# Down weights of the expert pairs issued from ACT's DMA queue, gate and up weights from SyncE's, in place of both from one queue

## What is computed

```python
def hier_moe(h, ...):     # 4 groups x 8 experts; top-1 group, then top-2 experts in it
    ...
    combine = jnp.sum(jax.nn.one_hot(eid, N_EXPERTS) * top_w[..., None], axis=1)
    a = jnp.einsum('cd,edf->cef', tc, w_g)      # w_g: 32 experts x 1024 x 256
    u = jnp.einsum('cd,edf->cef', tc, w_u)
    z = jax.nn.silu(a) * u * combine[..., None]
    return jnp.einsum('cef,efd->cd', z, w_d)    # w_d: 32 experts x 256 x 1024
```

## Time and profile before

| | before |
|---|---|
| median of 3 runs | 1402.3 us (1400.13 to 1407.38) |
| the profiled execution: its own time | 1399.06 us |
| its span, first to last instruction | 1397.4 us |
| PE busy | 1231.0 us, 88% |
| DVE, ACT, POOL busy | 586.8, 412.2, 239.1 us |
| DMA queue q1 (SP) | 281.57 MB, 52.5% of 16 engines' span |
| q0 (POOL), q10 (ACT) | 23.25 MB, 0.76 MB |
| mean granted PE clock | 0.961 |

### The profile page before, as it was taken

How to read it: one execution, slowest core, us unless ns; L and a number is a source line. 1 busy time by engine, 2 the same in 40 slices (tenths; PEclk the granted TensorE clock), 3 DMA queues, 4 the chain that set the end, 5 groups by cost and what they waited for, 6 DMA issues and landing times.

```text
span 1397.4 us, 18940 instructions
## 1 busy us (share of the span) xinstructions
PE 1231.0 (88%) x6424; PEld 809.6 (58%) x6425; DVE 586.8 (42%) x1353; ACT 412.2 (29%) x761; POOL 239.1 (17%) x183
## 2 busy tenths in 40 slices
PE   5999987999988998888499999789999889987871
PEld 5877766788876433333177777567888744332320
DVE  4467677333335222111254677753232442221115
ACT  5334444433342110001153443443332411110003
POOL 0314140022101111111003232301121011111100
PEclk9999999999999999999899999999999999998996
DMA  4423220453545999999533222105537289999995
GB/s 187 129 89 93 76 91 1 151 208 108 181 166 190 413 423 424 425 421 406 217 123 117 85 85 93 57 16 196 180 106 266 81 304 408 425 423 423 419 373 203
DMA packets 68192, 306.79 MB, mean 220 GB/s; under 512 B 11888, under 2 KB 11888, under 8 KB 56832
## 3 DMA queue, kind: packets, MB, share of 16 engines
q1 hardware_dynamic: 56960, 281.57, 52.5%
q0 software_dynamic: 10992, 23.25, 4.4%
q10 hardware_dynamic: 144, 0.76, 0.1%
HBM read 290.33 MB, written 23.07 MB: 224 GB/s over the span
## 4 chain that ended last, share of the span: by engine, by line
PE 60%; DMA 15%; SPq 7%; DVE 7%; issue 4%; ACT 3%; DVEq 2%; ACTq 0%; POOL 0%; POOLq 0%
PE bank L463 13%; PE bank L465 12%; PE bank L464 12%; PE bank L742 9%; DMA gu<-in_gu_w 9%; SPq L349 4%; PE bank L758 4%; SPq L354 3%; DMA raw<-in_stream 2%; PE bank L598 2%; DVEq L1186 2%; PE bank L737 1%; ACT prob L949 1%; PE bank L534 1%; DVE prob L1209 1%
## 5 line engine op out<-in xcount | busy, mean ns | idle before, releaser
L742 PE MATMUL bank<-gu,xgt 128*64 128x512 f32 x1024 | 242.4, 624 | 43.0 <-DMA gu<-in_gu_w 41.1
L463 PE MATMUL bank<-h_hi,w_hi 128*128 128x512 f32 x640 | 253.9, 397 | 6.6 <-DVE h_lo L1146 3.6
L465 PE MATMUL bank<-h_hi,w_lo 128*128 128x512 f32 x640 | 250.3, 391 | 0.0
L464 PE MATMUL bank<-h_lo,w_hi 128*128 128x512 f32 x640 | 249.8, 390 | 0.0
L742 PEld LDWEIGHTS bank<-gu,xgt 128*64 128x64 f32 x1024 | 75.6, 143 | 205.7 <-issue 188.7
L1104 DVE TENSOR_TENSOR w_lo<-raw,w_hi 128x1024 fp32r<-128x1024 f32 x102 | 128.0, 1255 | 149.6 <-ACT w_hi L868 148.6
L463 PEld LDWEIGHTS bank<-h_hi,w_hi 128*128 128x128 f32 x640 | 120.6, 188 | 33.0 <-DVE h_lo L1146 4.0
L465 PEld LDWEIGHTS bank<-h_hi,w_lo 128*128 128x128 f32 x640 | 120.5, 188 | 25.6
L464 PEld LDWEIGHTS bank<-h_lo,w_hi 128*128 128x128 f32 x640 | 120.6, 188 | 24.0
L868 ACT ACTIVATE w_hi<-raw 128x1024 fp32r<-128x1024 f32 x102 | 107.5, 1054 | 57.3 <-PE bank L465 57.3
L758 PE MATMUL bank<-dn,zt 128*64 128x512 f32 x512 | 117.2, 599 | 6.7 <-ACT zt L1065 3.2
(11 more groups left out here) (172 smaller groups left out, 1624.0 us busy)
## 6 DMA issues: line engine op xcount, KB each, us to landing
gu<-in_gu_w SPq DMA_DIRECT2D x18, 4096.0 KB, 33.2
raw<-in_stream SPq DMA_DIRECT2D x112, 512.0 KB, 3.3
dn<-in_dn_w SPq DMA_DIRECT2D x18, 2048.0 KB, 34.4
gu<-in_gu_w SPq DMA_DIRECT2D x24, 1024.0 KB, 19.5
dn<-in_dn_w SPq DMA_DIRECT2D x20, 1024.0 KB, 18.7
gu<-in_gu_w SPq DMA_DIRECT2D x32, 512.0 KB, 5.7
gu<-in_gu_w SPq DMA_DIRECT2D x8, 2048.0 KB, 24.3
swp<-pj SPq DMA_DIRECT2D x136, 64.0 KB, 2.0
```

The source lines that it names most:

```text
L463: mm(dst, ah, bh, start=start, stop=False)
L464: mm(dst, ah, bl, start=False, stop=False)
L465: return mm(dst, al, bh, start=False, stop=stop)
L742: last = mm(bank[b][e * CAP:(e + 1) * CAP, :], xgt[:, x_s, k, e * CAP:(e + 1) * CAP], gu[w_s][:, e, k, :], start=k == 0, stop=k == KD - 1)
```

## The change

SP no longer issues the down weights of pairs 3 to 15. ACT issues them instead: in its own loop over the pairs, behind the copy `zt` of pair n and before `y_half(n)`, it waits for dn_ok of pair n and issues the down weights of pair n + 3 (one DMA of 2 MB, or two of 1 MB for the pairs in PARTS). The buffers, the sizes, the semaphores that tell of the landing and the conditions under which a load may start are the same. The down weights of pairs 0 to 2 stay with SP.

```diff
@@ SP
-            def load_dn(l, p):
-                s = p % RING
-                sp.dma_start(dn[s]..., dn_w[...]).then_inc(dn_ld[s], 16)
...
                 load_gu_part(l, 3, 0)
                 sp.wait_ge(gu_ok, l * PAIRS + 1)
                 load_gu_part(l, 3, 1)
-                sp.wait_ge(dn_ok, l * PAIRS + 1)
-                load_dn_part(l, 3, 0)
-                load_dn_part(l, 3, 1)
                 for p in range(4, PAIRS):
                     sp.wait_ge(gu_ok, l * PAIRS + p - RING + 1)
                     ...
-                    sp.wait_ge(dn_ok, l * PAIRS + p - RING + 1)
-                    if p in PARTS:
-                        load_dn_part(l, p, 0)
-                        load_dn_part(l, p, 1)
-                    else:
-                        load_dn(l, p)
@@ ACT
+                def load_dn(p):
+                    if p in PARTS:
+                        for f in range(2):
+                            act.dma_start(dn[p % RING][:, :, f, :], dn_w[...]).then_inc(dn_part[p][f], 16)
+                    else:
+                        act.dma_start(dn[p % RING]..., dn_w[...]).then_inc(dn_ld[p % RING], 16)
                 for n in range(PAIRS):
                     ...
                     run(zt[:, :, :], ..., ACT.Copy).then_inc(zte_ok, 1)
+                    if n + RING < PAIRS:
+                        hold(act, dn_ok, n0 + n + 1)
+                        load_dn(n + RING)
                     y_half(n)
```

More of the change, by code:

```diff
@@ L340, in load_gu @@
                              gu_w[bass.ds(l * PAIRS + p, 1), :, :, :].rearrange("o e p n -> p (o e) n")).then_inc(gu_ld[s], 16)
-            def load_dn(l, p):
-                s = p % RING
-                sp.dma_start(dn[s][:, :, :, :].rearrange("p e k n -> p e (k n)"),
-                             dn_w[bass.ds(l * PAIRS + p, 1), :, :, :].rearrange("o e p n -> p (o e) n")).then_inc(dn_ld[s], 16)
             def load_gu_part(l, p, q):
@@ L1059, in y_half @@
                     run(yb[n % 2][:, 0:T], bank[4][:, :], ACT.Copy).then_inc(ya_ok, 1)
+                def load_dn(p):
+                    if p in PARTS:
+                        for f in range(2):
+                            act.dma_start(dn[p % RING][:, :, f, :], dn_w[bass.ds(l * PAIRS + p, 1), :, :, f * D:(f + 1) * D].rearrange(
+                                "o e p n -> p (o e) n")).then_inc(dn_part[p][f], 16)
+                    else:
+                        act.dma_start(dn[p % RING][:, :, :, :].rearrange("p e k n -> p e (k n)"),
+                                      dn_w[bass.ds(l * PAIRS + p, 1), :, :, :].rearrange("o e p n -> p (o e) n")).then_inc(dn_ld[p % RING], 16)
                 for n in range(PAIRS):
```

## The result

The median went from 1400.0 us (18 runs) to 1411.1 us (18 runs), a ratio of 1.0085 with a 95% interval of 1.0072 to 1.0098. The profiled execution went from 1399.06 to 1410.30 us, its span from 1397.4 to 1408.5. The forecast was +9.8 us, and both its sign and its size came about. Half of its reasoning was right; the profile after shows that the other half was not.

The account below looks back on a forecast made before the run. The prediction took the full-rate weight stream and PE's tail to bound each expert half. Its terms, 0 + 0 + 4.8 + 5.0 = +9.8 us, took 1402.3 to 1412.1 us, with a range of 1400.5 to 1421.

Parts of the forecast that it names:

- A full stream sets the end of the expert half: Expert halves: PE loses its lead and waits for weights; the end follows from the full-rate weight stream and PE's tail.
- SP's long issues are worth nothing: SP's queue: removing waits and 17 DMA issues a layer gains 0, since bytes issued sooner into a full stream land no sooner.
- ACT's issues cost 0.37 us each and do not stall: ACT, 13 turns a layer: 0.4 to 0.8 us before y_half, covered by silu's 4.36 us wait; 0 us.
- Two queues share, at the same rate: DMA engines: two weight queues interleave at an unchanged total rate, so the stream ends at 680.0 and 1364.3 as before.
- the 678 that the prediction named as a sign of being wrong: End of layer one's weight stream: the prediction is wrong if the stream ends before 678 us.
- The last landing moves to gate and up weights, with 7.5 us behind it: 4.8 + 5.0 us: Layer ends: gate and up weights land last, about 680.0 in place of 675.2 in layer one, before the whole tail; +9.8 us.
- Scatters: 0, with PE's lead as the cover: POOL's scatters in early pairs: silu late by 3.4 us a pair, some 15 us, taken from PE's lead; counted as 0.
- At most half as long again: POOL's scatter landings: turns for three queues in place of two stretch 15.5 us to at most 23.3.
- The mark named for the middle pairs: Expected sign in the profile after: longer waits for gate and up weights before pairs 7 and 8.
- if it is gone, up to 15 us a layer: Scatter term's exception: without PE's lead as cover, late scatters cost up to 15 us a layer.
- The sum: Whole kernel: 0 + 0 + 4.8 + 5.0 = +9.8 us, a median of 1412.1 us, +0.7%.

Follow-up runs that it names:

- e2: Kernel before, with POOL's scatter of pair n-4 put ahead of its gather of pair n: 1399.8 us, ratio 1.0006.
- e10: Kernel before, with the down weights of pair 15 alone issued from ACT's queue: 1410.3 us beside 1400.3, ratio 1.0078.
- e11: Changed kernel, down weights of pairs 13 to 15 back on SP and POOL's scatter ahead of its gather: 1402.2 us beside 1400.3, ratio 1.0015.
- e3: Changed kernel, with the down weights of pairs 13 to 15 back on SP behind their gate and up weights: 1413.2 us, ratio 1.0098.
- e1: Changed kernel, with POOL's scatter of pair n-4 put ahead of its gather of pair n: 1413.7 us, ratio 1.0104.
- e8: Kernel before, each whole gate-and-up load issued as two DMAs of 8 KB rows in place of one of 16 KB rows: 1402.8 us, ratio 1.0021.
- e9: Kernel before, without SP's wait for the first two gathers ahead of pair 2's last gate-and-up parts: 1410.5 us, ratio 1.0081.

## Why the prediction was right or wrong

- **A full stream sets the end of the expert half.** Right for the kernel before (e2, and e10's exact 10 us). In the changed kernel only layer one still meets that limit, within 0.2 us, with the scatters as late.
- **SP's long issues are worth nothing.** Nothing speaks against it: SPq went from 7% of the chain to 0%, and in e11, too, where it is 3%, there is no gain.
- **ACT's issues cost 0.37 us each and do not stall.** Right: 0.38 us, the longest of 34 took 0.63, and e11 shows no cost beyond its 3 us. That it is the small backlog, bounded by the three buffers of `dn`, that keeps them short is not shown.
- **Two queues share, at the same rate.** Right: the DMA share stays at 1.01 and the rate at 424 GB/s. It was not forecast that the stream would end a little sooner: its last landing is 1.4 us nearer to its start in layer one (245.6 us against 247.0) and 1.6 in layer two. At 677.7 us it is even just under the 678 that the prediction named as a sign of being wrong; 0.8 us of that are the earlier start, and why the rest came is not known.
- **The last landing moves to gate and up weights, with 7.5 us behind it: 4.8 + 5.0 us.** Right as a mechanism, shown alone in e10: +10.0, of which the profile has 5.1 and 4.7 in the two expert halves. In the changed kernel it accounts for less. Reckoned from each start, the last landing plus 7.5 us gives 253.1 and 250.8 us against 249.8 and 247.4 before, 3.3 + 3.4 = 6.7 us, since the stream ended sooner.
- **Scatters: 0, with PE's lead as the cover.** This is the step that failed, by its size and by its cover. "At most half as long again" counted queues as if their turns were alike. A turn is a packet: before, a packet of POOL's waited for one of q1's, sometimes of 16, sometimes of 8 KB; after, for one of 16 and one of 8 KB. The scatter took 29.1 us in place of 14.1, not 23.3 at most. The cover, PE's lead over the stream, was real but spent: at 17.3 us a pair PE fell behind the stream, waited for weights for 0.7 us in all, and ended layer two 3.6 us after what the landings allowed. The mark named for the middle pairs, longer waits for gate and up weights, did not come; they vanished. The prediction had named the case ("if it is gone, up to 15 us a layer"), took 0, and gave it no place among its rivals.
- **The sum** of +9.8 us came near to the measured 11 because both limits lie within 4 us of each other in each layer. They do not add: whichever is later counts, and each is enough by itself (e3, e10). Taking one away gave nothing (e1, e3). In that the number is partly luck: in the changed kernel the landings account for 6.7 us, and the rest is a wait that the forecast had put at 0.

Why e1 and e3 lie a little above the changed kernel is not settled; their intervals overlap its own.

## What to carry to other kernels

Where a stream of loads sets the end, the order in which the last loads land is worth as much as their bytes: what has the longest work behind it goes first, and a second queue takes that order away. Before a load goes to another queue, look at who else uses the DMA engines with small packets, since here each of its packets waited for one packet of every busy queue, whatever its size. And when undoing a suspect changes nothing, undo the other and then both before either is cleared.

## What the runs showed of the hardware

- The DMA engines took the queues in turn by packet: 170, 173 and 171 packets of three queues in 10 us, 125, 124 and 126 in 3 us where two of them have equal rows. The queue with rows of mostly 8 KB therefore got 1.36 MB beside the 2.52 MB of the one with rows of mostly 16 KB.
- With a second weight queue the landing time of POOL's transfers doubled, the scatters from 14.1 to 29.1 us, with the total rate unchanged. Halving the larger packets took ACT's waits for them from 242.9 to 58.9 us, and with one weight queue their landing from 14.0 to 10.4 us (e8).
- A DMA issue of SP's took up to 14.0 us while the DMA engines were full; one of ACT's, with 6 MB outstanding at most, never over 0.63 us.
- In e9 PE's granted clock was 0.64 on average at 455 to 460 us, behind a wait of 3.17 us, and 32 matmuls took 9.54 us in place of 7.09.
